# A decoder step on one core: two layer norms applied inside the stages that read their result

## The reference

```python
def layer_norm(x, g, b):
    mu = jnp.mean(x, -1, keepdims=True)
    var = jnp.mean(jnp.square(x - mu), -1, keepdims=True)
    return (x - mu) * lax.rsqrt(var + LN_EPS) * g + b

def swiglu(x, w_gate, w_up, w_down):
    return (jax.nn.silu(x @ w_gate) * (x @ w_up)) @ w_down

def ffn_half_step(x, w_gate, w_up, w_down, g, b):
    return layer_norm(DEEP_ALPHA * x + 0.5 * swiglu(x, w_gate, w_up, w_down), g, b)

def mixer_residual(x, att, gdn, w_o, g, b):
    return layer_norm(DEEP_ALPHA * x + jnp.concatenate([att, gdn], -1) @ w_o, g, b)

x = ffn_half_step(x, ffn1_w_gate, ffn1_w_up, ffn1_w_down, ln1_g, ln1_b)
q, k, v, qi, ki, wi, qkv, z, b_g, a_g = split(x @ w_in)     # 28 blocks of 128 columns or fewer
x = mixer_residual(x, attention(...), delta_rule(...), w_o, ln2_g, ln2_b)
x = ffn_half_step(x, ffn2_w_gate, ffn2_w_up, ffn2_w_down, ln3_g, ln3_b)
```

## Time and profile before

| | |
|---|---|
| median of 3 runs | 3067.73 us (3066.54 to 3073.72) |
| profiled execution | 3061.67 us |
| span of its trace | 3060.0 us, mean granted clock 0.949 |
| PE busy | 2774.4 us, 91% |
| DVE busy | 1537.6 us, 50% |
| ACT busy | 888.8 us, 29% |

### The profile page before, as it was taken

How to read it: one execution, slowest core, us unless ns; L and a number is a source line. 1 busy time by engine, 2 the same in 40 slices (tenths; PEclk the granted TensorE clock), 3 DMA queues, 4 the chain that set the end, 5 groups by cost and what they waited for, 6 DMA issues and landing times. The chain is left out here.

```text
span 3060.0 us, 44591 instructions
## 1 busy us (share of the span) xinstructions
PE 2774.4 (91%) x17300; PEld 2549.0 (83%) x17300; DVE 1537.6 (50%) x2425; ACT 888.8 (29%) x1458; POOL 268.1 (9%) x491
## 2 busy tenths in 40 slices
PE   6999999999949999968788788797879999999998
PEld 6999999999949789953588655466879999999998
DVE  5333333333444778847777578455353333333335
ACT  2111111111132457722355444352241111111113
POOL 0000000000500000005000000571000000000000
PEclk8999999999969999968899899898889999999999
DMA  3111111111231112225110201684111111111111
GB/s 109 56 42 42 42 42 43 48 42 49 63 111 36 43 65 71 93 72 132 42 42 18 58 15 32 187 237 123 27 42 56 42 53 43 41 46 43 41 41 59
DMA packets 266682, 190.40 MB, mean 62 GB/s; under 512 B 61520, under 2 KB 245024, under 8 KB 266503
## 3 DMA queue, kind: packets, MB, share of 16 engines
q1 hardware_dynamic: 213158, 111.80, 13.0%
q0 software_dynamic: 22656, 64.88, 6.6%
q10 hardware_dynamic: 30688, 11.27, 1.4%
HBM read 161.67 MB, written 26.22 MB: 61 GB/s over the span
## 5 line engine op out<-in xcount | busy, mean ns | idle before, releaser
L603 DVE TENSOR_TENSOR ffn_hidden<-ffn_hidden,ffn_ps_b 128x1092 f32<-128x1092 f32 x44 | 56.9, 1292 | 388.0 <-PE ffn_ps_b L85 388.0
L444 ACT ACTIVATE ffn_hi_d<-ffn_raw_d,ffn_row_mean 128x1024 fp32r<-128x1024 f32 x40 | 46.1, 1152 | 581.5 <-DVE ffn_row_mean L539 581.5
L460 ACT ACTIVATE ffn_h_hi<-ffn_hidden 128x1092 fp32r<-128x1092 f32 x44 | 49.3, 1120 | 485.7 <-DVE ffn_hidden L603 485.7
L238 POOL DMA_DIRECT2D ffn_raw_d<-in_ffn_w_down x40 | 21.3, 532 | 1580.0 <-DVE ffn_lo_d L548 1404.2
L85 PE MATMUL ffn_ps_a<-mixer_mix_hi,ffn_hi_g 128*128 128x364 f32 x528 | 117.5, 330 | 30.3 <-DVE ffn_lo_g L533 30.3
L85 PE MATMUL ffn_ps_a<-first_x_hi,ffn_hi_g 128*128 128x364 f32 x528 | 118.2, 332 | 10.2 <-DVE ffn_lo_g L533 5.9
L85 PEld LDWEIGHTS ffn_ps_a<-mixer_mix_hi,ffn_hi_g 128*128 128x128 f32 x528 | 91.8, 189 | 31.0 <-issue 30.5
L85 PE MATMUL ffn_ps_a<-first_x_lo,ffn_hi_g 128*128 128x364 f32 x528 | 116.8, 330 | 0.0
L85 PE MATMUL ffn_ps_a<-mixer_mix_lo,ffn_hi_g 128*128 128x364 f32 x528 | 116.7, 329 | 0.0
L85 PE MATMUL proj_ps_a<-first_x_hi,proj_w_hi 128*128 128x364 f32 x336 | 78.7, 343 | 41.9 <-DVE proj_w_lo L1122 41.9
L85 PE MATMUL ffn_ps_b<-first_x_lo,ffn_hi_u 128*128 128x364 f32 x528 | 116.6, 329 | 0.0
(11 more groups left out here) (709 smaller groups left out, 6962.0 us busy)
## 6 DMA issues: line engine op xcount, KB each, us to landing
ffn_raw_d<-in_ffn_w_down POOLq DMA_DIRECT2D x40, 512.0 KB, 3.8
proj_raw<-in_w_in SPq DMA_DIRECT2D x22, 512.0 KB, 3.8
second_ffn_raw_g<-in_ffn_w_gate SPq DMA_DIRECT2D x22, 512.0 KB, 4.3
second_ffn_raw_u<-in_ffn_w_up SPq DMA_DIRECT2D x22, 512.0 KB, 5.7
first_ffn_raw_g<-in_ffn_w_gate SPq DMA_DIRECT2D x21, 512.0 KB, 4.0
first_ffn_raw_u<-in_ffn_w_up SPq DMA_DIRECT2D x21, 512.0 KB
scratch_qkv<-proj_stage POOLq DMA_DIRECT2D x12, 544.0 KB, 3.0
delta_cur<-scratch_qkv SPq DMA_DIRECT2D x8, 768.0 KB, 5.5
```

The costliest lines, as they stand in the source:

```text
L238: eng.dma_start(dst, src).then_inc(raw_in[kind], 16)
L444: act.activation(d_hi[:, k, :], raw["d"][:, :], ACT.Identity, bias=row_mean[:, k:k + 1]).then_inc(whi_done["d"], 1)
L460: act.activation(h_hi[:, par, fb, :], act_buf[:, fb, :], ACT.Copy).then_inc(hhi_done, 1)
L603: dve.tensor_tensor(hid, hid, ps_b[:, :, 0:SL], ALU.mult).then_inc(mul_done, 1)
```

## The change

Both `apply_norm` stages go, and their work moves into the stages behind them, `project` and the second `ffn`.

- DVE scales a piece (`scale`), ACT writes `x_hi`, and DVE writes `x_lo` straight from the scaled residual, the bias and `x_hi` (`low`, now a scalar_tensor_tensor). ACT's second addition of the bias is taken off the way to `x_lo`.
- PE runs the first two weight blocks piece by piece, as `x_hi` and `x_lo` of each piece are made: step k does piece k of the first block and piece k - 2 of the second (`LAG`).
- In `project`, `res` gets its bias later, on ACT in rounds n = 2 and 3, four pieces each; POOL stores it then. `y`, `stage`, `sq` and `spill` now lie in the memory of `res`, and ACT and DVE wait at n = 7 (`INDEX_FROM`) until the stores are done; DVE clears `y` there. SP loads gain and bias, then the first two weight blocks, and the rope tables after them.
- In the second `ffn`, ACT scales `res` by ALPHA and adds ALPHA times the bias after the first hidden block's `weight_hi`, and DVE sums the residual behind the first hidden block. The means of slices 0 and 1 come after both hidden blocks, slice 2 halfway through the next gate block. `centre` runs three times behind `down_lo(0)`.
- Gain, bias and the first two weight blocks of the second `ffn` are loaded by POOL in `mixer_output`, behind the residual's eight loads. `rstd` of the second norm shares memory with the output rows.

```diff
@@ ffn, PE
+            def product(kind, ks):
+                return three_pass(pe, ps_a if kind == "g" else ps_b, ..., ks, start=0 in ks, stop=KT - 1 in ks)
+
+            def gates_as_x_comes():
+                pe.wait_ge(wlo_done["g"], 1)
+                pe.wait_ge(wlo_done["u"], 1)
+                for step in range(KT + LAG):
+                    if step < KT:
+                        pe.wait_ge(s["x_made"], step + 1)
+                        last = product("g", [step])
+                        if step == KT - 1:
+                            last.then_inc(gate_filled, 1)
+                    if step >= LAG:
+                        last = product("u", [step - LAG])
+                last.then_inc(up_filled, 1)
+                for kind, done in (("g", silu_done), ("u", mul_done)):
+                    pe.wait_ge(wlo_done[kind], 2)
+                    pe.wait_ge(done, 1)
+                    product(kind, range(KT)).then_inc(filled[kind], 1)
+                residual_means((0, 1))
+
+            def second_gates():
+                for fb in range(2):
+                    for kind, done in (("g", silu_done), ("u", mul_done)):
+                        pe.wait_ge(wlo_done[kind], 3 + fb)
+                        pe.wait_ge(done, 2 + fb)
+                        if fb == 0 and kind == "g":
+                            product(kind, range(KT // 2))
+                            residual_means((2,))
+                            product(kind, range(KT // 2, KT)).then_inc(filled[kind], 1)
+                        else:
+                            product(kind, range(KT)).then_inc(filled[kind], 1)
...
-            gates(0, 0, first=True)
-            with pe.Fori(0, CHUNKS // 2) as i:
+            if fresh is not None:
+                gates_as_x_comes()
+                second_gates()
+                down(0, 0)
+                gates(2, 0)
+                down(1, 1)
+            else:
+                gates(0, 0, first=True)
+            with pe.Fori(0 if fresh is None else 1, CHUNKS // 2) as i:
@@ ffn, ACT
+                    if first and fb == 0 and fresh is not None:
+                        act.wait_ge(s["shift_scaled"], 1)
+                        for k in range(KT):
+                            act.wait_ge(s["x_made"], k + 1)
+                            act.activation(res[:, k, :], res[:, k, :], ACT.Identity, scale=ALPHA,
+                                           bias=fresh.shift[:, k:k + 1]).then_inc(res_scaled, 1)
...
-            if weigh:
+            if fresh is not None:
                 for k in range(KT):
-                    act.activation(res[:, k, :], res[:, k, :], ACT.Copy, scale=ALPHA).then_inc(res_scaled, 1)
+                    act.wait_ge(s["x_scaled"], k + 1)
+                    act.activation(x_hi[:, k, :], res[:, k, :], ACT.Identity, bias=fresh.gb[:, 1, k:k + 1]
+                                   ).then_inc(s["x_hi_made"], 1)
@@ ffn, DVE
-                    if first:
+                    if first and fresh is None:
                         for i in (0, 1) if fb == 0 else (2,):
                             centre(i)
+                    if first and fresh is not None and fb == 0:
+                        sum_residual()
...
+            if fresh is not None:
+                scale(0)
             weight_lo("g", 0)
+            if fresh is not None:
+                scale(1)
             weight_lo("u", 0)
             dve.memset(eps[:, :], LN_EPS).then_inc(s["eps_set"], 1)
...
+                low(0)
+                for k in range(1, KT):
+                    if k + 1 < KT:
+                        scale(k + 1)
+                    low(k)
...
+                def centre_all():
+                    down_lo(0)
+                    for i in range(SLICES):
+                        centre(i)
+
+                per_chunk(dve, gates, down, centre_all)
@@ project, SP and POOL
+            column_load(sp, gb[:, 0, :], norm_g[0], s["gb_in"])
+            column_load(sp, gb[:, 1, :], norm_b[0], s["gb_in"])
             load(0)
+            load(1)
             sp.dma_start(cos[:, :], cos_in).then_inc(s["rope_in"], 16)
             sp.dma_start(sin[:, :], sin_in).then_inc(s["rope_in"], 16)
-            load(1)
...
+            for k in range(0, KT, 2):
+                pool.wait_ge(s["res_made"], k + 2)
+                pool.dma_start(resid_out[k:k + 2].rearrange("k p c -> p k c"), res[:, k:k + 2, :]
+                               ).then_inc(s["res_out"], 16)
@@ project, PE
+            pe.wait_ge(s["wlo_done"], 1)
+            for step in range(KT + LAG):
+                if step < KT:
+                    pe.wait_ge(s["x_made"], step + 1)
+                    product(0, step)
+                if step == LAG:
+                    pe.wait_ge(s["wlo_done"], 2)
+                if step >= LAG:
+                    product(1, step - LAG)
+            for n in range(2, n_blocks):
@@ project, ACT
+            x_high(0)
             weight_hi(0)
+            x_high(1)
             weight_hi(1)
+            for k in range(2, KT):
+                x_high(k)
...
+                if n in (2, 3):
+                    for k in range(4 * n - 8, 4 * n - 4):
+                        act.wait_ge(s["x_made"], k + 1)
+                        act.activation(res[:, k, :], res[:, k, :], ACT.Identity, bias=gb[:, 1, k:k + 1]
+                                       ).then_inc(s["res_made"], 1)
+                if n == INDEX_FROM:
+                    act.wait_ge(s["res_out"], 16 * KT // 2)
@@ project, DVE
-            step(dve.memset(y[:, :, :], 0.0))
...
+            dve.wait_ge(s["gb_in"], 32)
+            scale(0)
+            scale(1)
+            low(0)
             weight_lo(0)
-            weight_lo(1)
+            for k in range(1, KT):
+                if k + 1 < KT:
+                    scale(k + 1)
+                low(k)
+                if k == 1:
+                    weight_lo(1)
...
+                if n == INDEX_FROM:
+                    dve.wait_ge(s["res_out"], 16 * KT // 2)
+                    step(dve.memset(y[:, :, :], 0.0))
@@ mixer_output, POOL
             for m in range(KT):
                 pool.dma_start(res[:, m, :], res_in[m]).then_inc(s["res_in"], 16)
+            column_load(pool, gb[:, 0, :], g[0], s["gb_in"])
+            column_load(pool, gb[:, 1, :], b[0], s["gb_in"])
+            first(pool, s["first_in"])
+            pool.wait_ge(s["gb_in"], 32)
```

More of the change, by code:

```diff
@@ L8 @@
 from contextlib import ExitStack
+from dataclasses import dataclass
 import numpy as np
@@ L180, in halves_before @@
     return 2 * rows_before(g, own) + half * len(group) + group.index(t)
+@dataclass
+class Fresh:
+    gb: object
+    shift: object
+    rows: object
+    rstd: object
+LAG = 2
 def ffn(nc, name, w_gate, w_up, w_down, res, x_hi, x_lo, raws, ident, ones_mean, rstd_tok, rstd=None, weigh=False,
-        store=None, row_means=None):
+        store=None, row_means=None, fresh=None):
     with ExitStack() as ctx:
@@ new lines, in scale, with low @@
+            def scale(k):
+                dve.scalar_tensor_tensor(res[:, k, :], res[:, k, :], fresh.gb[:, 0, k:k + 1], fresh.rstd,
+                                         ALU.mult, ALU.mult).then_inc(s["x_scaled"], 1)
+            def low(k):
+                dve.wait_ge(s["x_scaled"], k + 1)
+                dve.wait_ge(s["x_hi_made"], k + 1)
+                dve.scalar_tensor_tensor(x_lo[:, k, :], res[:, k, :], fresh.gb[:, 1, k:k + 1],
+                                         x_hi[:, k, :].bitcast(F32), ALU.add, ALU.subtract).then_inc(s["x_made"], 1)
@@ L669, in column_load @@
         eng.dma_start(dst, vec.rearrange("(k p) -> p k", p=P)).then_inc(sem, 16)
[L672 to L704, removed]
-                dve.scalar_tensor_tensor(res[:, k, :], res[:, k, :], gb[:, 0, k:k + 1], rstd[:, :],
-                                         ALU.mult, ALU.mult).then_inc(s["scaled"], 1)
-            def low(k):
-                dve.wait_ge(s["hi_done"], k + 1)
-                dve.wait_ge(s["made"], k + 1)
-                dve.tensor_tensor(x_lo[:, k, :], res[:, k, :], x_hi[:, k, :].bitcast(F32), ALU.subtract)
-            dve.wait_ge(s["gb_in"], 32)
-            scale(0)
-            for k in range(1, KT):
-                scale(k)
-                low(k - 1)
-            low(KT - 1)
 HD = 64
@@ new lines, in decoder_step @@
+                    early.close()
+                    r = Scope(nc, keep, "main", side="right")
+                    k_t, ki_t = r.sb("k_t", [P, TP]), r.sb("ki_t", [P, TP])
+                    v_tok = r.sb("v_tok", [P, TILES, P])
+                    wi_tok = r.sb("wi_tok", [P, TILES, 8])
+                    beta, gate = r.sb("beta", [P, TILES, GH]), r.sb("gate", [P, TILES, GH])
+                    unit = r.sb("unit", [P, TILES, 8])
+                    qi_s = r.sb("qi_s", [P, 4, SAMPLE])
+                    scores_p = r.sb("scores_p", [P, sum(WIDTHS)])
@@ L3450, in decoder_step @@
                     raws, ident, ones_mean, rstd_tok, weigh=True,
```

(3 more changed lines are left out.)

123 lines of the change are left out of this document (70 added, 53 removed).

## The result

The kernel after takes **3037.53 us** (median of 4 runs, 3033.38 to 3042.6) where the kernel before took 3068.78 beside it (4 runs): ratio 0.991, 95% interval 0.9893 to 0.9927, that is 22 to 33 us less. The forecast was 3036.8 us. The profiled executions are 3061.67 us before and 3035.97 us after, 25.7 us apart. That is less than the 30.9 us of the sum, and most of what follows is about that difference.

A forecast was written before the change was run, and what follows sets the result against it. PE, busy 91% of the span, bounds the kernel, with two long waits at the serial norms. Projection 24.1 plus second feed-forward 6.8 gives 30.9 us; median 3067.73 less that is 3036.8 us, range 3030 to 3046.

The forecast's parts named there:

- the sum: Whole kernel: 24.1 us from the projection plus 6.8 from the second feed-forward, 30.9 us gained.
- The projection's start: Projection: PE's first matmul at 865.9 in place of 893.6, from DVE's scalings, low(0) and weight_lo(0).
- The wait ahead of block 2: Projection: new PE wait of 1.9 us, as DVE does weight_lo(2) only after three steps of rotating block 0.
- What I costed at nothing: ACT's bias instructions, the residual's stores on POOL, clearing y, later rope tables, ACT's scaling and the residual sum: all covered, 0 us.
- The rival of the late residual: Mixer's output: residual lands late behind the moved weight loads, up to 2.8 us, total 3039.6 us; 10%.
- The second feed-forward: PE starts 22.0 us earlier, first up block ends 21.7 earlier; less 13.0 stall and 1.9 clock, net 6.8 us.
- a stall of 13.0 us: Second feed-forward: PE waits ahead of the third mean for centre(0), which DVE reaches only after down_lo(0).
- the clock behind it: Second feed-forward: after PE's wait for centre(0), the clock restarts at 0.50 and costs 1.85 us; bounds 0 and 2.5.
- the mean itself: Second feed-forward: residual means on PE, two taking 1.22 us; the third needs centre(0).
- The step that failed: Behind both places PE runs without a gap, so what is won should reach the end unless a new wait arises.
- The rivals of the slow clock: Clock stays low in one stage's interleaved part, 3052 us, 5%; or in both stages and the block behind, 3085.4 us, 2%.

The follow-up runs named there:

- two kernels that take the stall away by reordering: Kernel after with DVE's three centrings ahead of down_lo(0), 3029.22 us; or only the first ahead, two inside the next chunk, PE's third mean a half block later, 3019.13 us.
- first half alone: Kernel before with only the projection's half of the change (first norm inside the projection); 3063.44 us, ratio to before 0.9995.
- first half alone, moved: Projection's half only, plus 17 PE instructions of already met waits in the projection's start; 3039.78 us, ratio to before 0.9915.
- second half alone: Kernel before with only the second norm moved inside the second feed-forward; 3064.25 us, ratio to before 0.9997.
- after, moved by 78: Kernel after plus 78 PE instructions of repeated waits in the projection's start, shifting the second loop; 3036.60 us, ratio to before 0.9907.
- second half, moved: Second feed-forward's half only, plus 70 PE instructions of repeated waits in the projection's start; 3062.79 us, ratio to before 0.9995.
- after, moved by 61: Kernel after plus 61 PE instructions of repeated waits in the projection's start; 3034.15 us, ratio to before 0.9892.
- first loop, moved by 28: Kernel after with centrings reordered, weight_lo(2) first, repeated waits of 28 instructions in token loading and 50 in the projection; 3018.26 us, ratio to before 0.9837.

## Why the prediction was right

**The projection's start** was forecast at 865.9 and came at 864.29, which is 865.92 when the 1.63 us are put back that the kernel was ahead anyway. The wait ahead of block 2 was 1.78 us (1.9), the gain 24.07 (24.1). Each came from durations of single instructions in the order of DVE's queue.

**What I costed at nothing** stayed at nothing: no wait on the residual's stores is in the trace, and the mixer's first wait is 15.1 us in two parts as before. The rival of the late residual is out too: the shift is 20.0 us when the mixer begins and 20.9 at 2181. The Trainium skill (DMA: Bandwidth & Descriptors, section "Issuing engines are not separate DMA queues") was weighed there, with up to 2.8 us, for its rule that DMAs of all engines interleave. The trace shows no such cost.

**The second feed-forward** was forecast with PE 22.0 us earlier at its start (30.29 - 7.96 = 22.33 from the copy), 21.7 at the first up block's end (22.05), a stall of 13.0 us (13.14), and 1.85 for the clock behind it (1.80). The one small miss is the mean itself, 0.97 us more on the slow clock. Net 5.9 in place of 6.8. The two kernels that take the stall away by reordering show that it is the named queue on DVE.

**The step that failed** is the sentence behind both places, that PE then runs without a gap and what is won should reach the end, "unless a new wait takes it back". I looked for the new wait on the other engines. There was one in PE's own instructions: 3.9 us along the loop in the kernel after, 3.5 of it at its three turns, and all of the first half's 22 us where that half stands alone. Nothing in my sum had a price for where a loop stands. With it, the sum for the kernel after is 24.1 + 5.9 - 3.9 = 26.1 us, and not 30.9. The pair of traces has 25.7; of that, 1.6 came before the change and 2.3 went in the scatter between the stages. The medians' 31.25 us in the first session and 28.0 in the second lie above it. The first interval, 22 to 33 us, holds both sums; the second, 21 to 30 us, holds 26.1 and not 30.9. So that the forecast came within 1 us of the median was partly luck: the median that it was counted down from, 3067.73, was 2 to 3 us higher than those of the kernel before in the later sessions, and the scatter is about as large as the missing term. The rivals of the slow clock did not come: PE reached the high clock within 5 us at both places.

## What to carry to other kernels

When a norm's pieces are fed to matmuls as they are made, the next thing late is whatever was queued behind the norm on the same vector engine; work it out by that queue, and move the first piece that PE needs ahead of bulk work. A change that adds or takes away a few matrix instructions ahead of a long loop can move the loop onto a bad place: look at the first matmul of each turn and at the instruction queue of both kernels before a gain or a loss is put down to the edit, and write the loop out if its gaps show. Instructions that only move a loop cost time too, some 0.11 us each here, where no other wait covers them. Halves of a change that each measure as nothing can still be worth 28 us together; a half's trace, stage by stage, shows which.

## What the hardware showed beyond that

At a turn PE's loop of 1756 instructions either has a gap or has none, and the gap comes with a fetch: of the 94 returns in the 13 traces with loops, 70 have a gap of 0.66 to 4.17 us and 8 or 9 packets on the queue of instructions, and 24 have neither. Which it is goes with where the loop starts in PE's compiled stream. It is not the start alone: the first loop, whose code is the same in these traces, starts at 770 in 12 of them and has one return without gap and packets in four.

| kernel | loop starts at | gaps at the turns, us |
|---|---|---|
| before | 19221 | none |
| first half alone | 19213 | 3.39 to 4.17 |
| first half alone, moved | 19230 | none |
| after, in five traces with the loop in its place | 20944 | 0.66 to 1.20 |
| second half alone | 20952 | 0.67 to 1.14 |
| after, moved by 78; second half, moved | 21022 | none |
| after, moved by 61 | 21005 | none |
| first loop, in 12 traces | 770 | 0.66 to 1.27, but none at one return in four of them |
| first loop, moved by 28 | 798 | 0.67 to 0.77 |

Counted in blocks of 256 the places do not sort: 13 is bad at 19213 and good at 21005, and 30 is good for the second loop and bad for the first. Counted in blocks of 255 they do: 95, 96, 105 and 112 have no gaps, and 5, 33, 34, 42 and 88 have them, the long ones at 88. A body of 1756 would then fit seven blocks from 29 or 30 neighbouring places only, and 95 to 112 lie within one such run. This count was found after the runs and none tested it; why a place a few instructions ahead of the good ones costs four times the others is open too.

The Trainium skill (Runtime: NRT & Kernel Launch, section "Instruction fetch mechanics") says that instructions are refilled in blocks of 256, with a marker put in at each block boundary, and that a taken branch out of the present window, two blocks there, costs a fetch; a marker that takes one of the 256 places would give the 255, which no run tested. The traces agree that such a branch can cost a fetch (0.7 to 4.2 us here, with 8 or 9 packets, 0.13 to 0.15 MB, and none with the loops written out). They do not agree with a window of two blocks: the loop of 1756 instructions, seven blocks, came round 24 times without a packet, and the measurement decides.
